# Expert rows gathered by token, and products that read the tokens from SBUF

## The reference, cut to what matters

```python
q = (hb @ w_query).reshape(PEER_BLOCK, PEER_HEADS, 2, KEY_HALF)
s1 = jnp.einsum('thd,hkd->thk', q[:, :, 0], sub_keys[0])
s2 = jnp.einsum('thd,hkd->thk', q[:, :, 1], sub_keys[1])
v1, i1 = lax.top_k(s1, PEER_TOPK)
v2, i2 = lax.top_k(s2, PEER_TOPK)
cand = (v1[..., :, None] + v2[..., None, :])         # 256 sums per head
cidx = (i1[..., :, None] * N_KEYS + i2[..., None, :])
best, sel = lax.top_k(cand, PEER_TOPK)
idx = jnp.take_along_axis(cidx, sel, axis=-1)        # 16 rows per token and head
gate = jax.nn.softmax(best, axis=-1)
ug = jnp.take(u_tab, idx, axis=0)
vg = jnp.take(v_tab, idx, axis=0)
act = jax.nn.gelu(jnp.einsum('td,thkd->thk', hb, ug), approximate=False)
return jnp.einsum('thk,thkd->td', gate * act, vg)
```

## Time and profile before

| what | us |
| --- | --- |
| median of three runs (3820.06 to 3827.55) | 3824.19 |
| span of the profiled execution | 4199.6 |
| of it, up to the expert stage | 904 |
| of it, the expert stage | 3296 |

### The profile page before, as it was taken

How to read it: one execution, slowest core, us unless ns; L and a number is a source line. 1 busy time by engine, 2 the same in 40 slices (tenths; PEclk the granted TensorE clock), 3 DMA queues, 4 the chain that set the end, 5 groups by cost and what they waited for, 6 DMA issues and landing times.

```text
span 4199.6 us, 38180 instructions
## 1 busy us (share of the span) xinstructions
PE 3314.8 (79%) x9348; PEld 1593.5 (38%) x9348; DVE 2313.6 (55%) x5821; ACT 950.0 (23%) x2161; POOL 2152.0 (51%) x2222
## 2 busy tenths in 40 slices
PE   8998989928777777877777777777777777887677
PEld 2454555513333333333333333333333333333222
DVE  2104552867755665555665655566555665556442
ACT  1003773312221221112112211211121121112111
POOL 0000300236566665666666666566666665666665
PEclk9999999969898898898888888888888888888888
DMA  9104102159999999999999999899999999999997
GB/s 357 64 15 126 32 19 113 61 188 352 344 357 359 353 359 354 347 368 343 341 359 347 350 356 344 332 354 355 360 347 358 358 357 348 343 363 358 361 362 303
DMA packets 365168, 1245.51 MB, mean 297 GB/s; under 512 B 52129, under 2 KB 57505, under 8 KB 362751
## 3 DMA queue, kind: packets, MB, share of 16 engines
q0 software_dynamic: 313504, 1141.02, 72.4%
q1 hardware_dynamic: 48852, 96.77, 6.6%
q10 hardware_dynamic: 2576, 5.10, 0.4%
HBM read 1220.34 MB, written 22.39 MB: 296 GB/s over the span
## 4 chain that ended last, share of the span: by engine, by line
PE 38%; issue 17%; another core or an unknown queue 9%; DVE 5%; DMA 4%; POOL 3%; ACT 1%; DVEq 0%; POOLq 0%; ACTq 0%; SPq 0%
PE ps_y L1692 33%; PE ps_q L950 5%; DMA urow<-in_u_tab,idx 3%; POOL urow L1473 2%; POOL vrow L1473 1%; DMA vrow<-in_v_tab,idx 1%; DVE urow L1612 1%; ACT diag L1580 1%; DVE aux L993 0%; PE ps_s L961 0%; DVE i L996 0%; DVE sel L996 0%; DVE i L992 0%; DVE aux L1029 0%
## 5 line engine op out<-in xcount | busy, mean ns | idle before, releaser
L1692 PE MATMUL ps_y<-vrow,diag 128*128 128x512 f32 (+1 forms) x4352 | 2220.8, 665 | 647.5 <-issue 329.9
L1612 DVE CUSTOM_DVE_ANT_0 urow<-urow,ps_h 128x1024 f32<-128x1024 f32 x1088 | 1299.8, 1220 | 1025.2 <-DMA urow<-in_u_tab,idx 865.6
L1692 PEld LDWEIGHTS ps_y<-vrow,diag 128*128 128x128 f32 (+1 forms) x4352 | 884.3, 209 | 1893.6 <-issue 1576.9
L1473 POOL DMA_INDIRECT vrow<-in_v_tab,idx x1088 | 1031.6, 948 | 785.7 <-issue 287.4
L1473 POOL DMA_INDIRECT urow<-in_u_tab,idx x1088 | 1030.7, 947 | 430.5 <-issue 282.8
L1580 ACT ACTIVATE diag<-const,wgt 128x128 f32<-128x128 f32 x1024 | 373.1, 396 | 1766.2 <-PE ps_y L1692 643.3
L950 PE MATMUL ps_q<-aux,w_q_sb 128*128 128x128 f32 x2048 | 271.7, 292 | 58.1 <-issue 49.4
L950 PEld LDWEIGHTS ps_q<-aux,w_q_sb 128*128 128x128 f32 x2048 | 263.9, 207 | 94.4 <-issue 93.2
L1293 POOL TENSOR_TENSOR xo<-xo,ot 128x1024 f32<-128x1024 f32 (+1 forms) x9 | 21.1, 2343 | 352.2 <-DVE ot L1249 352.2
L530 PE MATMUL ps_z<-hT,w_in_sb 128*128 128x512 f32 (+1 forms) x576 | 190.5, 491 | 4.6 <-DVE hT L448 4.6
L625 POOL MEMSET kTs<- 128x384 f32 x1 | 0.4, 418 | 322.7 <-POOLq L344 322.7
(11 more groups left out here) (181 smaller groups left out, 2341.3 us busy)
## 6 DMA issues: line engine op xcount, KB each, us to landing
ada<-in_w_ada SPq DMA_DIRECT2D x12, 2048.0 KB, 12.5
urow<-in_u_tab,idx POOLq DMA_INDIRECT x1088
vrow<-in_v_tab,idx POOLq DMA_INDIRECT x1088
w_in_sb<-in_w_in SPq DMA_DIRECT2D x8, 1024.0 KB, 17.9
w_q_sb<-in_w_query SPq DMA_DIRECT2D x8, 1024.0 KB, 14.3
x<-in_x_p ACTq DMA_DIRECT2D x8, 512.0 KB, 6.6
w_out_sb<-in_w_out SPq DMA_DIRECT2D x8, 512.0 KB, 7.0
xo<-in_x_p SPq DMA_DIRECT2D x8, 512.0 KB, 3.7
```

The lines of the kernel that those rows point to most:

```text
L1473: nc.gpsimd.indirect_dma_start(ring[k % RING][:, :], None, A[table][:, :], bass.IndirectOffsetOnAxis(ap=places[:, col:col + 1], axis=0)).t ...
L1612: nc.vector.tensor_tensor_reduce(out=urow[k % RING][:, :], in0=urow[k % RING][:, :], in1=ps_h[:, :], scale=1.0, scalar=0.0, op0=ALU.mult, ...
L1692: last = nc.tensor.matmul(ps_y[0:rows, c], diag[s % DIAGS][:, 0:rows], vrow[k % RING][:, c], start=(s == 0), stop=(s == PH * width(n) - 1))
```

## The change: what it does

**The v rows by token.** The row numbers of a tile are collected in `idxs` (128 tokens by 128 slots), transposed on PE (`places`, `by_slot`) and copied as integers to `idxT` (`take_places`, DVE). A gather of v then fetches all 128 slots of one token: partition s gets row `idxT[s, token]`. It runs one tile behind: body b gathers the u rows of tile b and the v rows of tile b-1, alternating, so there are ten bodies. Body 0 has 64 u gathers alone, body 1 has 128 u and 64 v, bodies 2 to 8 have 128 of each, body 9 has 128 v alone. The rings keep 8 buffers each.

**The sum over slots on PE.** The weights of a tile are collected in `wgt` (tokens by slots), transposed on PE, copied by ACT to `wgtT`. For every four tokens ACT writes their four weight columns into the column `MID` of cleared areas `place[:, z, i, 0:63]`, one small instruction for four tokens. A matmul's left operand is a window of 32 columns of that area in which the weight column stands at the token's place, and the other columns are zero; it adds the token's sum into one of 32 rows of `ps_y`. A `quad` is eight such matmuls (two halves by four tokens). The diagonal matrices are gone.

**The products from SBUF.** `h2n` has two buffers, and the product reads it there; `copy_h2` and `ps_h` are gone.

**The search in 17 steps.** Steps of the search for the next head stand behind the products of the head at hand, one behind each (two in tile 0), the last behind the whole. Step 15 raises `idx_ready`; it follows the head's last product. The search of head g+1 thus runs within head g, where before it ran a tile's worth of heads ahead.

**Tile 0.** Its transposes, queries and searches leave `output`; the first two heads' queries and the whole first search stand at the start of `experts`. All is written out, without a loop on the device.

```diff
 class Find:
+    STEPS = 17
+    def search(self, own, dve, g, step):
+        own.wait()
+        if step == 0:
+            dve.wait_ge(self.s_done, g + 1)
...
+        elif step == 15:
...
+                nc.vector.tensor_copy(self.idx[:, c], self.idxs[n % 2][:, c]).then_inc(self.idx_ready, 1)
+            own.add(nc.vector.reciprocal(self.gsum[:, :], self.gsum[:, :]))
...
+    def take_places(self, dve, n, v_used):
+        dve.wait_ge(self.idxT_tr, n + 1)
+        if n >= 2:
+            dve.wait_ge(v_used, v_slot(n - 1, 0))
+        nc.vector.tensor_copy(self.idxT[n % 2][:, 0:rows(n)], self.ps_t[:, 0:rows(n)])\
+            .then_inc(self.idxT_ready, 1)
 def output(nc, A, S):
-    heads = {2: [0], 3: [1], 4: [2], 5: [3], 6: [4], 7: [5], 8: [6, 7]}
...
-                for h in heads.get(t, []):
-                    find.search(own, dve, dve_passed, 0, h)
...
-            find.search(own, dve, dve_passed, 0, PH - 2)
             product(NTILE - 1)
-            find.search(own, dve, dve_passed, 0, PH - 1)
...
 def experts(nc, A, S):
-        diag = [sb(f"diag{i}", [P, P]) for i in range(DIAGS)]
-        h2n = sb("h2n", [P, D])
+        place = sb("place", [P, ZRING, 4, 2 * MID + 1])
+        wgt = sb("wgt", [P, SLOTS])
+        wgtT = sb("wgtT", [P, P])
+        h2n = [sb(f"h2n{i}", [P, D]) for i in range(2)]
...
+            def gather_u(n, s):
+                k, at = u_slot(n, s) % URING, (find.idx0 if is_sample(n) else find.idx)[:, s:s + 1]
+                if s % width(n) == 0:
+                    pool.wait_ge(idx_ready, find.known(head(n, s // width(n))))
+                if u_slot(n, s) >= URING:
+                    pool.wait_ge(u_used, u_slot(n, s) - URING + 1)
...
+            def gather_v(n, i):
+                t = token(n, i)
+                k, at = v_slot(n, i) % VRING, find.idxT[n % 2][:, t:t + 1]
+                if i == 0:
+                    pool.wait_ge(idxT_ready, n + 1)
+                if v_slot(n, i) >= VRING:
+                    pool.wait_ge(v_used, v_slot(n, i) - VRING + 1)
...
+            def put(n, c):
+                q, j = n * QUADS + c, rows(n) // QUADS
+                if q >= ZRING:
+                    act.wait_ge(v_used, quad_end(q - ZRING))
+                nc.scalar.activation(place[:, q % ZRING, 0:j, MID],
+                                     wgtT[:, 0:rows(n)].rearrange("p (j c) -> p j c", j=j)[:, :, c], ACT.Copy)\
+                    .then_inc(placed, 1)
...
-                    nc.vector.tensor_tensor_reduce(out=urow[k % RING][:, :], in0=urow[k % RING][:, :], in1=ps_h[:, :],
+                nc.vector.tensor_tensor_reduce(out=urow[s % URING][:, :], in0=urow[s % URING][:, :], in1=h2n[n % 2][:, :],
...
+            for step in range(find.STEPS):
+                find.search(own, dve, 0, step)
+            for b in range(NU):
...
+                    for k in range(w):
+                        product(b, h, k)
+                        if g + 1 < NU * PH:
+                            for step in range(each * k, each * (k + 1)):
+                                find.search(own, dve, g + 1, step)
...
-                    last = nc.tensor.matmul(ps_y[0:rows, c], diag[s % DIAGS][:, 0:rows], vrow[k % RING][:, c],
-                                            start=(s == 0), stop=(s == PH * width(n) - 1))
+                    for i in range(j):
+                        s = v_slot(n, j * c + i)
+                        last = nc.tensor.matmul(ps_y[QUADS * i:QUADS * (i + 1), cols],
+                                                place[:, z, i, MID - c:MID - c + QUADS], vrow[s % VRING][:, cols],
+                                                start=(c == 0), stop=(c == QUADS - 1))
+                        if half:
+                            last.then_inc(v_used, 1)
```

More of the change, by code:

```diff
@@ L874, in _, with rows, u_slot, v_slot @@
                 assert own.n == PER, (own.n, PER)
+NU = NT + 1
+URING = 8
+VRING = 8
+ZRING = 8
 def is_sample(n):
-    return isinstance(n, int) and n == 0
+    return n == 0
 def width(n):
     return TOPK // 2 if is_sample(n) else TOPK
[L886 to L895, removed]
+def rows(n):
+    return DEC if is_sample(n) else P
+def u_slot(n, s):
+    return s if is_sample(n) else SLOTS // 2 + SLOTS * (n - 1) + s
+def v_slot(n, i):
+    return i if is_sample(n) else DEC + P * (n - 1) + i
+def head(n, h):
+    return n * PH + h
 class Find:
-    PASS = 28
     def __init__(self, nc, S, stack):
@@ L983, in top16 @@
         nc = self.nc
[L985 to L995, removed]
@@ new lines, in take_places, with by_slot @@
+    def take_places(self, dve, n, v_used):
+        nc = self.nc
+        dve.wait_ge(self.idxT_tr, n + 1)
+        if n >= 2:
+            dve.wait_ge(v_used, v_slot(n - 1, 0))
+        nc.vector.tensor_copy(self.idxT[n % 2][:, 0:rows(n)], self.ps_t[:, 0:rows(n)])\
+            .then_inc(self.idxT_ready, 1)
+def by_slot(nc, n, bank, c0, tile, ident):
+    if not is_sample(n):
+        return nc.tensor.transpose(bank[:, c0:c0 + P], tile[:, :], ident)
+    for half in range(2):
+        p = slice(DEC * half, DEC * (half + 1))
+        last = nc.tensor.matmul(bank[p, c0:c0 + DEC], tile[p, 0:DEC], ident[p, p], start=True, stop=True,
+                                skip_group_check=True)
+    return last
@@ L1468, in _ @@
+            store(NU - 1)
+            sp.wait_ge(y_out, 16 * NU)
         @block.gpsimd
         def _(pool):
-            def gather(table, ring, full, n, h, k):
-                col = width(n) * h + k
-                places = idx0 if is_sample(n) else idx
-                nc.gpsimd.indirect_dma_start(
-                    ring[k % RING][:, :], None, A[table][:, :],
-                    bass.IndirectOffsetOnAxis(ap=places[:, col:col + 1], axis=0)).then_inc(full[k % RING], 16)
-            def start():
-                pool.wait_ge(idx_ready, known(0, 0))
-                for k in range(width(0)):
-                    gather("u_tab", urow, u_full, 0, 0, k)
@@ new lines, in weights @@
+            def weights(g):
+                n, h = divmod(g, PH)
+                w = width(n)
+                dve.wait_ge(gelu_done, g + 1)
+                if h == 0 and n:
+                    dve.wait_ge(wT_tr, n)
+                own.wait()
+                nc.vector.tensor_tensor(wgt[:, w * h:w * (h + 1)],
+                                        (find.gate0 if is_sample(n) else find.gate)[:, w * h:w * (h + 1)],
+                                        gelu[g % 2][:, 0:w], ALU.mult).then_inc(w_ready, 1)
@@ L1638, in finish @@
                 nc.vector.tensor_tensor(y[r, :], y[r, :], x1[r, :], ALU.add).then_inc(y_done, 1)
-            FINISH = 5
-            AHEAD = 2
-            PER = PH * find.PASS + FINISH
-            def start():
-                products(0, 0)
-                weights(0, 0)
-                dve.wait_ge(g2_in, 48)
-                for i in range(2):
-                    own.link(nc.vector.tensor_tensor(g2[i][:, :], g2[i][:, :], gpost[:, :], ALU.mult))
-                assert own.n == AHEAD, own.n
@@ L1697, in body @@
+            find.transposes(pe, 0, h2n, h2_in, wT_ready, ident)
+            pe.wait_ge(S["w_q_full"], 16 * (KC + 1))
+            for g in range(2):
+                find.queries(pe, g)
+                find.scores(pe, g)
+            for b in range(BODIES):
                 for h in range(PH):
-                    if more:
+                    g = head(b, h)
+                    if b:
                         if h == 0:
-                            transposes(n + 1)
-                        find.queries(pe, n + 1, h)
@@ L1702, in body @@
-                    if h == 0 and not is_sample(n):
-                        pe.wait_ge(y_free, n)
-                    for k in range(width(n)):
-                        add_row(n, h, k)
-                        if k == width(n) // 2 - 1 and more:
-                            find.scores(pe, n + 1, h)
-            run(pe, lambda: None, body, lambda: None)
+                            take_weights(b - 1)
+                        quad(b - 1, 4 * h)
+                    if h == PH - 1 and b < NU:
+                        find.places(pe, b, ident)
```

599 lines of the change are left out of this document (292 added, 307 removed).

## The result

The kernel after takes 4363.23 us (4343.94 to 4371.57) against 3822.12 us: a ratio of 1.1408, interval 1.1379 to 1.1436. It is slower, as forecast, by 14.1% instead of 8.2%, and above the stated range of 3750 to 4300. Its profiled execution has a span of 4357.0 us, which is a run like the others; that of before, 4199.6 us beside runs of 3820, was not. The forecast took its excess for something that every profile adds, and scaled its sum down by it; that made 102 of the 228 us by which it fell short, and terms of the sum itself made the other 126.

The account below looks back on a forecast made before the run. Two close floors were taken to bound the kernel, POOL at 2.49 and transfers at 2.56 us a gather pair. Terms 866 + 216 + 320 + 2617 + 198 + 20 = 4237, times 0.976, gave 4135 us; range 3750 to 4300.

Parts of the forecast that it names:

- the factor: Last step, from sum to runs: 0.976, remote waits taken as the profiler's, the rest as evenly stretched; 4237 became 4135.
- The likeliest case: The forecast itself, 4135 us, 8% slower, chance 0.42; its own range 4060 to 4260 us.
- (c): Rival: the profile stretches everything alike, 0.9106; 4237 gives 3858 us, 0.9% slower; chance 0.14.
- (d): Rival: even stretch, transfers keep up with POOL, 2.49 us a gather pair; 3759 us, 1.7% faster; chance 0.18.
- (e): Rival: even stretch, gather pair 2.56 us, rounds cancel with the waits gone; 3813 us, about no change; chance 0.07.
- D: Bodies 2 to 8, 56 heads: each one round, 15 gather pairs of 2.62 plus 7.44, 46.74 us; 2617 us.
- E: Body 9, 128 v gathers without u: the ring of 8 makes gathers wait for quads; 198 us, the tail 20 more.
- A: Up to the first gather: 65 us saved before the expert stage, new serial prologue 27; first gather at 866 us.
- B: Body 0, 64 u gathers: DVE bounds, two search steps to a product; 27 us a head, 216 us.
- C: Body 1: first row, 16 products, a search and tile work make 40 us a head; 320 us.
- (a): Rival: products hold no gather, gather pair 2.56 us; 4087 us; chance 0.10.
- (b): Rival: every phase occurs, products hold gathers 0.49 us a pair, pair 2.98; 4431 us; chance 0.09.

Follow-up runs that it names:

- after_psum: The kernel after, with the products reading h2 from PSUM again (two ACT copies per tile): 4213.41 us, ratio 1.1026.

## Why the prediction was wrong

**The step that failed**, and that put the measured time out of the range, is the last one, from the sum to the runs. It took the "remote" waits for the profiler's, the rest for evenly stretched, and multiplied 4237 by 0.976. The second profile of before shows neither: its span and its runs agree, as they do for all seven other kernels run here, and the excess of the first was nearly all idle time of POOL. The sum was already in the time of the runs. Without the factor it reads 4237 us, 2.9% below 4363; with it 4135, 5.2% below. The likeliest case's own range, 4060 to 4260, is 4160 to 4365 without the factor and just holds the measured time. With every term right and the factor kept, the forecast would have been 4357 x 0.976 = 4252, 2.5% below. The factors of rivals (c), (d) and (e), 0.9106, rest on the same reading and fall with it, and with them the chance given to a faster kernel.

**The terms, by their own steps.** The factor made 102 of the 228 us of the miss, and the terms made more. Their mechanisms were right in D and E, and one size was wrong in both: 5.0 to 5.2 us for a row to land, read off an empty queue.

- A, the first gather: 859.4 us, forecast 866. Tiles of `output` follow each other at 15.5 us (755.09 and 770.61 in the trace of after), taken as 15.7.
- B, body 0: 181 us, forecast 216. DVE bounds, as said. A head takes 22.6, not 27: the first product comes 4.5 us after the first gather instead of 5.2, the next gather 0.27 after the cast instead of 0.8, and products and steps up to the cast take 17.9 where the sum had 21.0 for products, search and weights; the gate, for one, is made while the next head's first row is on its way.
- C, body 1: 327 us, forecast 320, near by luck. The sum had DVE busy without a break behind the first row. DVE waited 109.0 us for rows there; the held gathers, 1.160 us (u) and 1.287 (v), set the pace, and without the holding body 1 takes 293 us (`after_psum`).
- D, bodies 2 to 8: the mechanism was right, both sizes low. The product of a head's last u row begins 6.7 us after that row's gather, in the mean of 56 heads, where the sum had 5.21; it ends 0.4 before the next head's first gather, where the sum had 1.0. From the last u gather to the next head's first it is 8.4 us instead of 7.44, and POOL's wait is 5.9 a head, not 5. The pair was 2.72, not 2.62, above the 2.68 that the case's range allowed: the phase with a hold of 0.08 is reached by few products where every head restarts. Together 2.4 us a head, 136 in all, more than the 120 by which the sum fell short, since B was 35 too high.
- E, body 9 with the tail: 237 us, forecast 218. A quad begins 6.5 us after the gather of its last row, in the mean, where the sum had 5.0. And POOL went on only 0.25 after a whole quad (4210.27 + 3.36, 4213.88), where the sum let it go on after 0.65 of one; quads ran in 1.92 to 3.64 us.

**The rivals.** (a), products that hold no gather, is refuted twice: the operand in SBUF costs 235 us in the kernel before, and 150 in the kernel after. The inference of the Trainium skill ("SBUF — State Buffer", section "Who interferes with whom") that `tensor_tensor` leaves descriptor generation alone does not carry over to this product, whose gathers take up to 1.99 us for 0.94; the rule of the same section on two SBUF inputs does. (b), a hold of 0.49 a pair, was too much: it is 0.22 here (0.988 + 1.117 against 2 x 0.94), and more (0.37) only in the kernel before, where products bunch behind a search.

**What the change exchanged.** Bound by transfers before, 1.01 of their time; by a round of product, search step and gather after, 0.92. The search cut in steps was not what cost, but that its last step came behind the last product of the head before. Put one head earlier, the same steps stand beside heads of 42.0 us, no longer than those of the kernel before (42.65).

## What to carry to other kernels

Compare the span of a profile with the runs before building on its waits: an execution 10% longer than its runs shows the pace of instructions rightly and the bound wrongly, and its idle times must not be scaled into a forecast. Where a queue runs in order and its transfers are the bound, what tells the next transfers must be known well ahead (here one head earlier was enough), for a wait at the head of each group costs the latency every time, and a lead within the queue bought it back only once per body. An operand moved from PSUM to SBUF is free only if no other engine is held up by it: look at what a second engine does while the instruction runs. And a landing time read off an empty queue is too short for a row that has others before it: here 5.0 to 5.2 us became 6.5 to 6.7.

## What the runs showed of the hardware

- A gather that begins inside a DVE product with two SBUF operands ends about 0.8 us after that product (0.78 to 0.84 for all but 3 of the 649 such gathers of over 1 us in after), also where the next product follows at once: 1.99 instead of 0.94 us each, so that back-to-back products nearly halve POOL's pace. With one operand in PSUM gathers take 0.94 beside the same products.
- The cost of such holding went with the phase: 0.37 us a pair of gathers where products bunch behind a search (before with SBUF), 0.22 with a restart per head (after), 0.15 with the search ahead, the last hidden behind transfers of 404 GB/s.
- Four float32 matmuls into four strips of 32 columns ran side by side: the 16 records of a quad took 1.92 us at a granted clock of 1.00, the level of 2.4 GHz (4201.76 to 4203.68 in after), where 16 records of 128 columns took 7.03 at 1.00. At 0.50, the level of 1.2 GHz, a quad took 3.64 (4323.47 in after).
- The granted clock was 0.63 to 0.68 by stage in after against 0.91 in the second profile of before: between the two levels, the lower one for much of the time. PE had gaps between quads in after (6.58 us in the rows of body 9). In bodies 2 to 8 POOL waited 19.8 us in all for PE, so there the clock cost little; in body 9, where POOL waits for whole quads, it is part of each round.
